# Loading rounded high parts by DMA, gate products in quadrants, and the attention heads two groups later

## The reference, cut to what matters

```python
h   = rmsnorm(x, norm1_g)
proj = h @ w_in + b_in                       # q | k | v | xr | yr | gate logits
attn = block_attention(rope(rmsnorm(q)), rope(rmsnorm(k)), v)      # 8 query heads, 2 key heads
xc   = depthwise_conv(xr)                     # 4 taps
# rglru, once forward and once backward, 16 diagonal blocks of 64 channels:
r = sigmoid(block_diag(xc, wa)); i = sigmoid(block_diag(xc, wi))
log_a = 8 * r * log_sigmoid(lam); a = exp(log_a)
u = sqrt(-expm1(2 * log_a)) * (i * xc); h_t = a_t * h_{t-1} + u_t
rec = (forward + backward) * gelu(yr)
mix = sigmoid(g_A) * (attn @ w_attn_o) + sigmoid(g_R) * (rec @ w_lru_o)
x = x + mix @ w_out
x = x + moe(rmsnorm(x))                       # top 4 of 32 experts, clamped SwiGLU
out = rmsnorm(x, final_g)
```

## Time and profile before

| what | value |
|---|---|
| median of three runs | 1163.36 us |
| profiled execution, span | 1161.2 us |
| around the span (median less span) | 2.16 us |
| TensorE busy | 1081.6 us (93%) |
| VectorE busy | 382.9 us (33%) |
| ScalarE busy | 234.2 us (20%) |
| GpSimd busy | 0.2 us |
| DMA, mean | 379 GB/s |

### The profile page before, as it was taken

The page is one execution under the profiler, slowest core; times in us unless marked ns, Lnnn a source line. Parts: engine busy times, 40 slices in busy tenths (PEclk is TensorE's granted clock), DMA queues, the critical chain, the costliest instruction groups (busy, mean ns, idle before and its releaser), DMA issues.

```text
span 1161.2 us, 13145 instructions
## 1 busy us (share of the span) xinstructions
PE 1081.6 (93%) x5391; PEld 502.8 (43%) x5391; DVE 382.9 (33%) x671; ACT 234.2 (20%) x371; POOL 0.2 (0%) x4
## 2 busy tenths in 40 slices
PE   5998999989999999999998989898989898989997
PEld 5998789823333333333333323332333233323332
DVE  6996798532322222222121212121211212121122
ACT  5388843100111111111111111111110101010112
POOL 0000000000000000000000000000000000000000
PEclk9999999989999999999999999999999999999999
DMA  8543146998999999999999999999999999999996
GB/s 351 186 171 145 73 160 278 418 400 333 429 397 425 431 425 429 428 428 429 428 429 428 430 428 427 430 428 428 430 428 428 429 428 430 428 427 429 429 428 248
DMA packets 32618, 439.89 MB, mean 379 GB/s; under 512 B 3760, under 2 KB 3888, under 8 KB 5712
## 3 DMA queue, kind: packets, MB, share of 16 engines
q1 hardware_dynamic: 32112, 438.53, 89.9%
q10 hardware_dynamic: 480, 0.99, 0.2%
HBM read 438.46 MB, written 1.05 MB: 378 GB/s over the span
## 4 chain that ended last, share of the span: by engine, by line
PE 61%; DMA 33%; DVE 4%; ACT 1%; issue 1%; SPq 0%; DVEq 0%
DMA slot<-in_w_gu_dram 27%; PE ps L1333 25%; PE ps L1037 12%; PE ps L1342 10%; DMA slot<-in_w_down_dram 6%; PE ps L1305 4%; PE ps L1286 3%; PE ps L1300 1%; PE ps L1387 1%; DVE slot_r L627 1%; PE ps L1092 1%; PE ps L1135 1%; PE ps L1264 1%; PE ps L1156 1%; PE ps L1365 0%
## 5 line engine op out<-in xcount | busy, mean ns | idle before, releaser
L1333 PE MATMUL ps<-slot,lru 128*64 128x512 f32 x880 | 198.9, 595 | 21.0 <-DMA slot<-in_w_gu_dram 20.7
L1342 PE MATMUL ps<-slot,lru 128*64 128x512 f32 x896 | 203.3, 596 | 14.8 <-DMA slot<-in_w_down_dram 14.3
L1333 PE MATMUL ps<-slot,qT 128*64 128x512 f32 x880 | 202.1, 601 | 14.4 <-DMA slot<-in_w_gu_dram 12.9
L1333 PEld LDWEIGHTS ps<-slot,lru 128*64 128x64 f32 x880 | 62.7, 137 | 147.6 <-issue 113.5
L1333 PEld LDWEIGHTS ps<-slot,qT 128*64 128x64 f32 x880 | 62.5, 137 | 147.1 <-issue 134.9
L1342 PEld LDWEIGHTS ps<-slot,lru 128*64 128x64 f32 x896 | 62.3, 137 | 135.4 <-issue 117.1
L558 ACT ACTIVATE lru<-ps 128x512 f32<-128x512 f32 x32 | 19.1, 598 | 419.7 <-PE ps L1333 419.7
L993 DVE TENSOR_TENSOR lru<-ps,cst 128x1024 f32<-128x1024 f32 x32 | 39.2, 1225 | 141.5 <-PE ps L1387 141.5
L970 DVE TENSOR_SCALAR lru<-sq,x_sb,small 128x64 f32<-128x64 f32 x66 | 17.7, 312 | 188.1 <-PE ps L1286 188.1
L1037 PE MATMUL ps<-wide_r,slot_r 128*128 128x256 f32 x492 | 66.2, 286 | 0.2 <-DVE slot_r L627 0.2
L1305 PE MATMUL ps<-lru 128*128 128x512 f32 x136 | 63.9, 593 | 0.9 <-DVE lru L1017 0.9
(11 more groups left out here) (212 smaller groups left out, 905.1 us busy)
## 6 DMA issues: line engine op xcount, KB each, us to landing
slot<-in_w_gu_dram SPq DMA_DIRECT2D x110, 2048.0 KB, 34.9
slot<-in_w_down_dram SPq DMA_DIRECT2D x55, 2048.0 KB, 33.2
wide<-in_w_gu_dram SPq DMA_DIRECT2D x15, 2048.0 KB, 34.8
slot<-in_pre_dram SPq DMA_DIRECT2D x14, 2048.0 KB, 8.3
wide<-in_w_down_dram SPq DMA_DIRECT2D x8, 2048.0 KB, 35.3
slot<-in_w_lru_dram SPq DMA_DIRECT2D x2, 1024.0 KB, 13.3
wide<-in_w_gu_dram SPq DMA_DIRECT2D x2, 1024.0 KB, 14.8
late<-in_w_gu_dram SPq DMA_DIRECT2D x1, 2048.0 KB, 16.8
```

The source lines that it names most:

```text
L1333: ins = nc.tensor.matmul(ps[64 * side:64 * side + 64, 4 + b, :], xgT[i % 2][:, k, :], rows[r][:, o:o + BANK], start=(k == 0), stop=(k == K ...
L1342: ins = nc.tensor.matmul(ps[64 * side:64 * side + 64, bank, :], actT[(i - 1) % 2][:, k, :], w[:, r, side * BANK:(side + 1) * BANK], start= ...
```

## The change: what it does

1. **High parts of chunks 2 to 11** are no longer made by ScalarE or VectorE. GpSimd issues a second DMA of the same chunk from memory, into the tile of the high part, whose type is fp32r. For chunks 3 to 11 it waits for the same count as SyncE's load of the chunk; for chunk 2 until chunk 1 has landed. The low part waits for both loads. Chunks 0, 1, 12, 13 and 14 stay with ScalarE.
2. **Gate products in quadrants.** Each 128 x 128 product with two diagonal blocks becomes two 64 x 64 products. For the forward direction (m = 0, 1) they sit in the upper left and lower right quarter of the array; for the backward one (m = 2, 3) they read a copy of xc whose two halves of 64 partitions are exchanged (`xc_other`) and sit in the other two quarters. SyncE makes the copy with two DMAs for each unit, behind the loads of chunks 4 and 6, and loads the gate weights in three DMAs instead of one. ScalarE now waits for all products of a block before it reads them.
3. **Order.** Unit 0's blocks stand one each ahead of groups 8 and behind groups 8, 9 and 10. The q/k transposes come behind group 15 instead of 13. Unit 1's blocks stand behind groups 20 to 23, the heads start at group 20 instead of 18. On ScalarE unit 1's decays move from groups 20 to 22 to groups 24 to 26, its root from 24 to 27; the q/k root stands between the gates of blocks 2 and 3. On VectorE the low parts of chunks 6, 7, 8, 9 and 10 and the pieces of unit 1 stand in new places.

```diff
+        xc_other = gA
-        CAST_V = (5, 9)
+        CAST_A = (0, 1, 12, 13, 14)
+        UNIT1_AT, HEADS_AT = [20, 21, 22, 23], 20
...
+            def load_lru_weights(u):
+                w_sb = ring[LOWS][:, KD * TOK:]
+                sp.dma_start(w_sb[:, 0:1024], w_lru[u][:, 0:1024]).then_inc(lruw_in, 16)
+                for r in range(2):
+                    sp.dma_start(w_sb[64 * r:64 * r + 64, 1024:], w_lru[u][64 - 64 * r:128 - 64 * r, 1024:]
+                                 ).then_inc(lruw_in, 16)
...
+                if c in (4, 6):
+                    u = 0 if c == 4 else 1
+                    sp.wait_ge(conv_ok, 4 * u + 4)
+                    for r in range(2):
+                        sp.dma_start(xc_other[64 * r:64 * r + 64, 4 * u:4 * u + 4, :],
+                                     xc[64 - 64 * r:128 - 64 * r, 4 * u:4 * u + 4, :]).then_inc(xc_moved[u], 16)
...
-            lru_gates(0, range(4))
+            lru_gates(0, range(2))
+            for i in range(8, 10):
+                group(i)
+            lru_gates(0, [2])
             act.wait_ge(qk_inv, 1)
             nc.scalar.activation(qk_rstd, qk_rstd, ACT.Sqrt).then_inc(qk_rs, 1)
-            split_high(6)
-            for i in range(8, 14):
+            lru_gates(0, [3])
+            lru_decay(0, 0)
+            for i in range(10, 16):
...
-                if 20 <= i < 23:
-                    lru_decay(1, i - 20)
-                if i == 24:
+                if 24 <= i < 27:
+                    lru_decay(1, i - 24)
+                if i == 27:
                     lru_root(1)
...
+        @block.gpsimd
+        def _(pool):
+            for c in range(PRE):
+                if c in CAST_A:
+                    continue
+                if c >= PAIRS:
+                    pool.wait_ge(*CONSUMED[c - PAIRS])
+                else:
+                    pool.wait_ge(*landed(c - 1))
+                pool.dma_start(high(c), pre[c, :, 0:WIDTH[c]]).then_inc(high_in[c % PAIRS], 16)
...
-                if s == 0:
-                    split_low(7)
-                if s == 2:
+                if s == 1:
                     split_low(8)
                 if s == 3:
+                    split_low(9)
+                if s == 4:
                     lru_input(1)
-                if s == 5:
+                if s == 6:
                     lru_square(1)
-                if s == 6:
-                    split_high(9)
-                    split_low(9)
                 if s == 7:
                     lru_scaled(1)
                 if s == 8:
                     lru_scan(1)
-                    split_low(10)
                 if s == 9:
                     lru_sum(1)
                     recurrent_branch()
                 if s == 10:
+                    split_low(10)
                     recurrent_split()
...
-                pe.wait_ge(lruw_in, 16 * (u + 1))
+                pe.wait_ge(lruw_in, 48 * (u + 1))
+                pe.wait_ge(xc_moved[u], 32)
...
+                    if c >= 1:
+                        pe.wait_ge(gate_read, 4 * c)
+                    for k in range(2):
+                        for m, src in ((k, xc), (2 + k, xc_other)):
+                            for r in range(2):
+                                rows, o = slice(64 * r, 64 * r + 64), 64 * r if m < 2 else 64 - 64 * r
+                                ins = nc.tensor.matmul(half(6 + m // 2, k)[o:o + 64, :], lru_w_sb[rows, m, c % 4, o:o + 64],
+                                                       src[rows, c, :], start=True, stop=True)
+                    ins.then_inc(gate_ps, 4)
...
-            lru_gate_products(0, range(4))
-            for i in range(8, 14):
+            lru_gate_products(0, [0])
+            for i in range(8, 16):
                 group(i)
+                if i < 11:
+                    lru_gate_products(0, [i - 7])
```

More of the change, by code:

```diff
@@ L182, in encoder_layer @@
         lruw_in = sem("lru_weights_in")
+        xc_moved = [sem(f"xc_halves_moved{u}") for u in range(2)]
         split_hi, split_lo = sem("chunk_high"), sem("chunk_low")
+        high_in = [sem(f"chunk_high_in{i}") for i in range(PAIRS)]
         h_hi, h_lo, rec_split, attn_split = (sem(n) for n in ("h_high", "h_low", "rec_split", "attn_split"))
@@ L248, in encoder_layer, with high_landed @@
         IN_CHUNK, Q_CHUNK, BR_CHUNK, MIX_CHUNK = [0, 1, 4, 5, 6, 7, 8, 9], 2, [10, 11, 13], [12, 14]
-        CAST_V = (5, 9)
+        CAST_A = (0, 1, 12, 13, 14)
+        UNIT1_AT, HEADS_AT = [20, 21, 22, 23], 20
         def casts_before(c):
-            return 2 * sum(b not in CAST_V for b in range(c))
+            return 2 * sum(b in CAST_A for b in range(c))
+        def high_landed(c):
+            return high_in[c % PAIRS], 16 * sum(b % PAIRS == c % PAIRS for b in range(c + 1) if b not in CAST_A)
         WIDTH = [KD * 2 * KVW if c == Q_CHUNK + 1 else CH for c in range(PRE)]
@@ L465, in _ @@
                 group(i)
[L466 removed]
             for i in range(4, 8):
                 group(i)
[L469 to L472 removed]
+            lru_gates(0, range(2))
+            for i in range(8, 10):
+                group(i)
+            lru_gates(0, [2])
             act.wait_ge(qk_inv, 1)
             nc.scalar.activation(qk_rstd, qk_rstd, ACT.Sqrt).then_inc(qk_rs, 1)
[L475 to L476 removed]
+            lru_gates(0, [3])
+            lru_decay(0, 0)
+            for i in range(10, 16):
                 group(i)
[L478 removed]
+                if i % 2 == 1 and i < 14:
                     lru_decay(0, i // 2 - 4)
             copy_qk()
[L481 to L482 removed]
             lru_root(0)
@@ L627, in low_part @@
                 return nc.vector.tensor_tensor(dst, whole, hi.bitcast(f32), ALU.subtract)
-            def split_high(c):
-                dve.wait_ge(*landed(c))
-                link(high_part(high(c), whole(c)))
             def split_low(c):
-                if c not in CAST_V:
+                if c in CAST_A:
                     dve.wait_ge(split_hi, casts_before(c) + 2)
+                else:
+                    dve.wait_ge(*landed(c))
+                    dve.wait_ge(*high_landed(c))
                 low_part(low(c), whole(c), high(c)).then_inc(split_lo, 1)
```

40 lines of the change are left out of this document (12 added, 28 removed).

## The result

Five runs of the changed kernel have a median of 1170.54 us (1170.15 to 1171.79), five of the kernel before 1163.36 us (1162.69 to 1167.68): a ratio of 1.0053 with a 95% interval of 1.0041 to 1.0066. The change makes the kernel 0.5% slower. The forecast was 1169.0, with slower given a chance of 0.51.

The account below looks back on a forecast made before the run. The chain to the branch start, not DMA, was taken to bound the first 168 us, and its shift to reach the end: 1163.4 + 3.9 (late recurrence) + 1.7 (clock) = 1169.0 us, range 1160 to 1178.

Parts of the forecast that it names:

- A shift of the start: Branch products begin at 167.81 us in the kernel before; any shift of that was carried one to one to the end.
- Step 4: Second unit and heads, 88 to 168 us: heads 2 us early, unit 1's recurrence late, branches at 171.7, +3.9 us.
- Step 1: High parts by DMA: loads at 426 GB/s, chunk plus high part 9.8 us after issue plus some 2, price 0.
- my own three signs that the prediction is wrong: Branches start before 168 us, gate blocks keep 1.7 us, or low parts wait for DMA.
- my upper bound: For the high-part loads: they move half as fast, so chunk plus high part takes some 15 us.
- Rival (c): Rounding loads are slow: at half rate +18 us, 1181; at three quarters some 1172; chance 0.12.
- Rival (d): Loads do not round or are cheap copies: times as forecast, only the output would tell; within the remaining 0.03.
- Step 2: Quadrant gate products: four run together, a block takes 0.87 us instead of 1.97; 1.73 if only pairs.
- Rival (b): Quadrants only pair up: seven blocks cost 0.87 us more each, head 6 on 6.1 us later, 1175; chance 0.17.
- Step 3: First unit, 55 to 88 us: group 8 starts at 59.5, 4.0 us won; group 16 starts 1.2 us earlier.
- Step 5: TensorE's clock: 8 us idle before the branches likely halves it for 3.3 us, +1.7 us, bounds 0 and 3.2.
- Rival (a): Recurrence not late, TensorE sets the branch start at 163.3 to 163.5, no clock loss: 1159; chance 0.13.

Follow-up runs that it names:

- e8: Changed kernel with chunk 7 loaded ahead of unit 1's gate weights on SyncE's queue: 1168.99 us.
- e1: Changed kernel with unit 1's decays on ScalarE at groups 23 to 25 and its root at 26, one group earlier: 1163.51 us.
- e3: Kernel before with GpSimd's rounding loads of the high parts of chunks 2 to 11 alone, all else in the old order: 1164.19 us.
- e2: Changed kernel with the high parts of chunks 2 to 11 made by ScalarE and VectorE again, without GpSimd loads: 1180.82 us.
- e4: Changed kernel with full 128x128 gate products again, no moves of the halves, a unit's gate weights in one load: 1172.07 us.
- e9: Changed kernel with unit 1's decays at groups 23, 23, 24, root at 25, VectorE's recurrence steps earlier, low part 10 at head step 5: 1159.12 us.
- e10: e9 and e8 together: early recurrence, low part 10 at head step 5, chunk 7 ahead of unit 1's gate weights: 1156.95 us.
- e7: Changed kernel with 40 throwaway products on TensorE between group 31 and the branches: ratio 1.0044 to the kernel before.
- e11: Kernel before with the gate part alone (quadrants, moves, split weight load, unit 0's blocks between groups 8 to 11): 1166.32 us.

## Why the prediction was right, and where it was not

- **A shift of the start goes one to one to the end: right.** +8.95 at the start, +8.8 in the span.
- **Step 4, the recurrence of unit 1 placed too late: right, and the main cause.** From head 6's scores to the branches I had 36.7 us (135.0 to 171.7), the trace has 35.8, in e8 too; before it was 30.7. The two waits stand where they were named, 4.48 us before the square and 5.04 us before the scaling; the root ended at 156.8, 5.3 us later than forecast, with head 6 5.9 us late. TensorE waits 3.85 us before head 7's transposes (4.5) and 6.40 us before the branches (8). e1 undoes it by one index.
- **Step 4, heads 2 us early: wrong, they were 3.8 late.** 5.9 us were missing. 4.4 of them are not in e8: 0.6 for group 8's start, mostly low part 4's wait of 0.46 us on its rounded copy, and 3.85 for chunk 7 with the clock's fall behind its wait. The other 1.4 us, which e8 has too, are small change: a group behind a gate block or scores takes 3.07 to 3.13 us to the next piece, and I had 2.88 for most. Without chunk 7's part, in e8, the branches start at 172.34; forecast 171.7.
- **Step 1, price 0 for the loads: this step failed.** The rate was right, the landing was not, and "low parts wait for DMA" was one of my own three signs that the prediction is wrong. It came: low part 5 waits 4.06 us (at no visible cost: e1 and e3 wait 3.24 and 2.94 us there and are level with the kernel before), low part 7 5.98. A rounded copy takes 14.4 us to land (median), not 9.8 + 2 but near the 15 us of my upper bound, as its data starts 4 to 5 us after the issue. And chunk 7 took 21.65 us: I had checked when SyncE could issue it, but not what lay ahead of it in its queue. Rival (c), a slow rate, did not come: 20 MB in 4.2% of the span of all 16 engines. Rival (d) cannot be told from the times, as low parts take 4.42 us either way. The 6.8 us estimated from the Trainium skill ("DMA: Bandwidth & Descriptors", Anatomy of one DMA) fit no load of this stretch, where two queues shared the engines: even chunk 3's copy of 1 MB took 10.2 us.
- **Step 2, quadrants: right in kind.** Sixteen quadrant instructions take 1.02 us, 0.064 each, where a full one has 0.22: four at once. The sum used about 1.0 us a block and not its own unit of 0.87, and 1.0 is what it took. By the Trainium skill ("TensorEngine Tiling (Array Packing)", Gotcha 1) row tiles cannot reach one PSUM bank at the same time; here both row halves of a product write one bank, and the trace does not show the 1.73 us that this would give. Rival (b) is out.
- **Step 3: right for TensorE.** Group 8 starts at 60.17 (59.5), 3.4 us won over 63.54. VectorE's wait of 2 us for the q/k root did not come; low part 5's wait on DMA stands there.
- **Step 5, +1.7 for the clock: right in its place, wrong in the sum.** The piece behind the start took 1.84 us longer. But the kernel before falls some 96 us behind its start, the profiled execution of the changed one does not, and the rest is the same. I added the new loss and did not ask what becomes of the old one; in e2, e4 and e8 both came.
- **Rival (a), TensorE sets the start, 1159**: what the change could have had. e9 and e10 have its mechanism, at 1159.1 and 1157.0.

The sum came within 1.5 us because its errors stood against each other: +5.9 for heads that came late, -0.8 in the recurrence and -1.9 for the clock make +3.2 in the profiled execution, which lies 1.25 us above the median of its kernel and has 0.4 us less around its span. The kind and place of the main loss were foreseen; that the number was so close is luck.

## What to carry to other kernels

Where several engines take turns, look first at which chain releases the next stage, and place its passes by when their inputs are ready: here one index on ScalarE was worth 7 us, and work taken off an engine was worth 0 or 10 us depending on that order. When a load is moved, ask not only when it is issued but what stands ahead of it in its queue and how fast that moves. A clock loss counted for one version has to be looked for in the other too.

## What the runs showed of the hardware

- A load that GpSimd issues from float32 in memory into an fp32r tile moves at the plain rate: 19.92 MB in 4.2% of 1170 us, some 405 GB/s. In the changed kernel's records of single transfers its first data came 3.8 to 5.3 us after the issue, where SyncE's queue, when idle, needed about 1 us. While both queues had work each moved about half (2.87 and 2.67 MB from 58 to 71 us).
- Beside the rounding loads, loads and moves in rows of 4 KB held the engines at 277 GB/s with all of them busy, against 418 at 84 to 103 us. In the same records a transfer of 4 KB took about 0.25 us and one of 16 KB 0.63, so 16 against 26 GB/s an engine; the whole weight load of e4, in 8 KB pieces, had 0.32 us for each. Two of these three weight loads and all the moves also cover only 64 partitions; no run separates that from the row length.
- The clock after the same wait differs between executions: behind 2.73 to 2.74 us of idleness of TensorE group 8 took 3.13 us in e7 and e8 and 5.49 in e1, e2 and e11. A wait makes a fall possible, not certain.
